# An expert step with its bias products first and the next rows' gather between the halves of gate and up

## The chip, the cores and the metric
The kernel runs on one core of a Trainium2 chip. The metric is the device time of one execution in microseconds. Of the kernel before, three timed executions gave 1781.65 us as the median (1779.54 to 1782.54). A separate, profiled execution took 1782.32 us.

## The reference
The reference is two transformer blocks over 256 tokens of width 1024, in float32. The first block mixes the tokens by four recurrent branches, normalises, and then runs a mixture of experts; the second block is a dilated attention with a pooling branch. The change touches only the experts:

```
gu = xb @ w_gu + b_gu                    # rows of one expert, 1024 -> 2048
gate, up = gu[:, :1024], gu[:, 1024:]
gate = minimum(gate, 7); up = clip(up, -7, 7)
glu = gate * sigmoid(1.702 * gate)
y = ((up + 1) * glu) @ w_down + b_down   # 1024 -> 1024
out[token] += weight * y                 # each token goes to 4 of the 32 experts
```

All 32 experts are run, each on the rows of the tokens that chose it (at most 64 rows in one step). An expert has 8 MB of gate and up weights and 4 MB of down weights, and each weight is read from HBM once.

## The kernel before, in words
The order of the work is written out by hand for each engine, with semaphores between them. TensorE (PE), VectorE (DVE), ScalarE (ACT) and SyncE's DMA queue (SP) each run their own loop over 32 expert steps `i`. Steps 0, 1 and 2 are written out on PE; steps 3 to 7, 8 to 23 and 24 to 31 are loops. Steps 8 to 23 carry an extra piece each, `embed` (line 1347), a product of the first block's gating that has nothing to do with the expert. Between steps 25 and 26 stands `expert_bias` (line 1324).

PE's step (lines 1350 to 1406) is, in its order:
1. the gate and up products, line 1360: for `k` 0 to 7, four matmuls (two banks, two column halves of the array). `k` 0 to 3 read weight room 0, `k` 4 to 7 room 1, each of 4 MB. After every second `k` the semaphore `gu_used` is raised;
2. the bias products, line 1367: four small matmuls of 32 rows that pick the expert's bias out of the table `BGU` by a one-hot `ESEL`; they close the sums and raise `gu_full`;
3. `scatter`, line 1337: the rows of the step before are added to their tokens in four banks;
4. `gather`, line 1311: the rows of the next expert are picked out of `x1` by a one-hot `PICK`, into `x_bank`;
5. two transposes of `PICKW` (line 1382), the next scatter's table;
6. four transposes of the hidden rows `GH` (line 1386), which wait for `h_ready`;
7. `turn_rows`, line 1318: four transposes of the gathered rows `XR`, into the up bank;
8. the down products, line 1399, on rooms 2 and 3 (2 MB each), which wait for `hm_ready`, and in steps 8 to 23 `embed`.

DVE's part (lines 2435 to 2455) picks the one-hots for later gathers and scatters early in the step, then waits for `gu_full` and works the activation: minimum of the gate (2443), clip of the up half (2444), the next `ESEL` (2445), the product with the sigmoid (2447), the last product (2448), which raises `h_ready`; then it copies `PTW` (2450). ACT (lines 1786 to 1800) does the sigmoid (1788), copies the gathered rows to `XR` (1790), the turned hidden rows to `HM` (1792), which raises `hm_ready`, the turned gathered rows to `XG` (1794) and the result rows to `YSB` (1796).

SP issues the four weight transfers of a step in the order of the rooms 0, 1, 2, 3, each once its room is free: room 0 when `k` 3 of the step before is done, room 1 when `k` 7 is, room 2 after the first half of the down products, room 3 after the second (line 539). In the first two refills (line 535) rooms 0 and 1 come by halves.

Of the kernel before, what the change touches and what calls it, by code (L numbers as in the profile page):

```python
# [16 lines left out]
KD = D // P  # L17
W = 512
# [6 lines left out]
EXPERTS = 32  # L25
CAP = 64
# [175 lines left out]
def build(nc, ins, consts, outs):  # L202
    stack = ExitStack()
    with stack:
# [6 lines left out]
        def sig(name):  # L211
            if name not in signals:
                signals[name] = stack.enter_context(nc.semaphore(name.replace(" ", "_")))
            return signals[name]
# [136 lines left out]
        ESEL = room(at, CAP)[0:2 * EXPERTS]; at += CAP  # L351
# [10 lines left out]
        BGU = room(at, D)[0:2 * EXPERTS]; at += D  # L362
# [20 lines left out]
        gate_bank, up_bank, y_bank, x_bank = small_bank  # L383
# [298 lines left out]
        def _(pe):  # L682
# [72 lines left out]
            for m in range(2):  # L755
                for k in range(KD):
                    if k % 4 == 0 and m == 0:
                        pe.wait_ge(sig(f"first_in_{k // 4}"), 32)
                    mm = pe.matmul(ps[:, m * T:m * T + T], w[:, k, m * P:m * P + P], XT[:, k, :], start=k == 0, stop=k == KD - 1)
# [12 lines left out]
            for nm, wt in (("gx", WX), ("ga", WAD)):  # L772
                for i in range(2):
                    ps = small(f"D {nm} {i}")
                    for m in range(2):
                        mm = pe.matmul(ps[:, m * T:m * T + T], wt[:, 2 * i + m, :], xc[:, 2 * i + m, :], start=True, stop=True)
# [7 lines left out]
            for k in range(KD):  # L784
                mm = pe.matmul(ps[0:8, 0:T], w[:, k, :], XT[:, k, :], start=k == 0, stop=k == KD - 1)
# [13 lines left out]
            for i in range(2):  # L799
                ps = small(f"C row {i}")  # L800
                for m in range(2):
                    mm = pe.matmul(ps[:, m * T:m * T + T], c("headrow", (2 * i + m) * P, (2 * i + m + 1) * P)[0:4, :], gC, start=True, stop=True)
                mm.then_inc(sig("small_full"), 1)
            ps = small("C col")
            for n, r in enumerate((uC, mC)):
                for j in range(TT):
                    mm = pe.transpose(ps[:, 8 * n + 4 * j:8 * n + 4 * j + 4], r[:, j * P:j * P + P], ident[0:4, 0:4])
# [13 lines left out]
            for j in range(TT):  # L821
                ps = small(f"C num {j}")
                for h in range(4):
                    if j == 0:
                        mm = pe.matmul(ps[:, h * P:h * P + P], sC[:, h, 0:P], vC[:, 0, h * P:h * P + P], start=True, stop=True)
                    else:
                        pe.matmul(ps[:, h * P:h * P + P], sC[:, h, P:T], vC[:, 0, h * P:h * P + P], start=True, stop=False)
                        mm = pe.matmul(ps[:, h * P:h * P + P], sC[:, h, T:T + P], vC[:, 1, h * P:h * P + P], start=False, stop=True)
                mm.then_inc(sig("small_full"), 1)
            ps = small("C den")  # L830
            for h in range(4):
                pe.matmul(ps[:, h:h + 1], sC[:, h, 0:P], c("ones", 0, 1), start=True, stop=True)
                pe.matmul(ps[:, 4 + h:5 + h], sC[:, h, P:T], c("ones", 0, 1), start=True, stop=False)
                mm = pe.matmul(ps[:, 4 + h:5 + h], sC[:, h, T:T + P], c("ones", 0, 1), start=False, stop=True)
# [31 lines left out]
            for l in range(8):  # L866
# [3 lines left out]
                elif l == 6:  # L870
                    ps = small("B level 6")
                    for n in range(8):
                        j, h = divmod(n, 4)
                        e = eBs[0][:, h, j * P:j * P + P]
                        mm = pe.matmul(ps[0:CH, n * CH:n * CH + CH], e[:, 0:CH], e[:, CH:P], start=True, stop=True)
                    mm.then_inc(sig("small_full"), 1)
                else:
                    ps = small("B cross")
                    for h in range(4):
                        mm = pe.matmul(ps[:, h * P:h * P + P], eBs[1][:, h, 0:P], eBs[1][:, h, P:T], start=True, stop=True)  # L880
# [426 lines left out]
            def gather(bank):  # L1307

                for j in range(TT):
                    for half in range(2):  # L1310
                        mm = pe.matmul(bank[CAP * half:CAP * half + CAP, :], PICK[:, j, :], x1[:, j, half * W:half * W + W],  # L1311
                                       start=j == 0, stop=j == 1, skip_group_check=True)
                return mm
# [36 lines left out]
            def expert_step(i, tile, before=None):  # L1350


                pe.wait_ge(sig("xg_ready"), i + 1)
                for k in range(KD):
                    if k % 4 == 0:
                        pe.wait_ge(sig(f"expert_in_{k // 4}"), 16 * i + 64 if before is None else 32 * i + 32)
                        w = expert_room(k // 4)
                    for n, bank in enumerate((gate_bank, up_bank)):
                        for half in range(2):
                            mm = pe.matmul(bank[CAP * half:CAP * half + CAP, :], XG[:, k % 4, k // 4, :], w[:, k % 4, n * D + half * W:n * D + half * W + W],  # L1360
                                           start=k == 0, stop=False, skip_group_check=True)
                    if k % 2:
                        mm.then_inc(sig("gu_used"), 1)
                pe.wait_ge(sig("esel_ready"), i + 1)
                for n, bank in enumerate((gate_bank, up_bank)):
                    for half in range(2):
                        mm = pe.matmul(bank[CAP * half:CAP * half + CAP, :], ESEL[EXPERTS * n:EXPERTS * n + EXPERTS],  # L1367
                                       BGU[EXPERTS * n:EXPERTS * n + EXPERTS, half * W:half * W + W], start=False, stop=True, skip_group_check=True)
                mm.then_inc(sig("gu_full"), 1)
                if before != 0:  # L1370
                    if before == 1:
                        pe.wait_ge(sig("proj_out"), proj_no("pp 3") + 1)
                    pe.wait_ge(sig("y_ready"), i)
                    pe.wait_ge(sig("ptw_ready"), i + 1)
                    scatter(first=before == 1)
                pe.wait_ge(sig("pick_ready"), i + 2)
                if tile is not None:
                    pe.wait_ge(sig("ple_sig"), i - 7)
                gather(x_bank).then_inc(sig("gathered"), 1)
                pe.wait_ge(sig("pickw_ready"), i + 1)  # L1380
                for j in range(TT):
                    mm = pe.transpose(y_bank[:, j * P:j * P + P], PICKW[:, j, :], ident)
                mm.then_inc(sig("ptw_full"), 1)
                pe.wait_ge(sig("h_ready"), i + 1)
                for m in range(4):
                    mm = pe.transpose(gate_bank[:, m * P:m * P + P], GH.rearrange("s (p k) -> s p k", k=4)[:, :, m], ident)
                mm.then_inc(sig("ht_full"), 1)
                pe.wait_ge(sig("rows_ready"), i + 1)
                turn_rows(up_bank).then_inc(sig("rows_turned"), 1)
                pe.wait_ge(sig("ptw_ready"), i + 2)  # L1390
                pe.wait_ge(sig("hm_ready"), i + 1)
                for u in range(2):
                    pe.wait_ge(sig(f"expert_in_{2 + u}"), 16 * i + 16)
                    if before == 1 and u == 0:
                        pe.wait_ge(sig("extra_in"), 16)
                    for m in range(4):
                        w = extra if before == 1 and u == 0 and m < 3 else expert_room(2 + u)
                        for half in range(2):
                            mm = pe.matmul(y_bank[CAP * half:CAP * half + CAP, :], HM[:, m, u, :], w[:, m, half * W:half * W + W],  # L1399
                                           start=u == 0 and m == 0, stop=u == 1 and m == 3, skip_group_check=True)  # L1400
                    if u == 0:
                        mm.then_inc(sig("down_used"), 1)
                mm.then_inc(sig("y_full"), 1)
                if tile is not None:
                    pe.wait_ge(sig("ple_in"), 32)
                    embed(i, tile)
# [489 lines left out]
        def _(dve):  # L1896
# [529 lines left out]
            def expert_step(i, tile):  # L2426
                link = [0]

                def then(ins_):

                    link[0] += 1
                    ins_.then_inc(sig("expert_chain"), 1)
                    dve.wait_ge(sig("expert_chain"), LINKS * i + link[0])

                e, nxt = i % EXPERTS, (i + 1) % EXPERTS
                dve.wait_ge(sig("ptw_full"), i + 1)
                pick(PICKW, e, "pickw_ready", True)
                dve.wait_ge(sig("pickw_ready"), i + 1)
                then(TS(rank[:, :, bass.ds(e, 1)], rank[:, :, bass.ds(e, 1)], -float(CAP), None, ALU.add))
                dve.wait_ge(sig("gathered"), i + 1)  # L2440
                pick(PICK, nxt, "pick_ready", False)
                dve.wait_ge(sig("gu_full"), i + 1)
                TS(GH, gate_bank[:, :], 7.0, None, ALU.min).then_inc(sig("g_ready"), 1)  # L2443
                then(TS(UH, up_bank[:, :], 7.0, -7.0, ALU.min, ALU.max))
                dve.tensor_copy(ESEL, c("eye32")[0:2 * EXPERTS, bass.ds(nxt, 1)].to_broadcast([2 * EXPERTS, CAP])).then_inc(sig("esel_ready"), 1)
                dve.wait_ge(sig("sig_ready"), i + 1)
                then(TTn(GH, GH, SGH, ALU.mult))
                STT(GH, UH, 1.0, GH, ALU.add, ALU.mult).then_inc(sig("h_ready"), 1)
                dve.wait_ge(sig("ptw_full"), i + 2)
                dve.tensor_copy(PTW, y_bank[:, 0:T]).then_inc(sig("ptw_ready"), 1)  # L2450
                assert link[0] == LINKS
                if tile is not None:
                    dve.wait_ge(sig("ple_sig"), i - 6)
                    v = base[:, tile, bass.ds((i % 8) * P, P)]
                    TTn(v, v, SGP, ALU.mult).then_inc(sig("ple_mul"), 1)  # L2455
# [198 lines left out]
```

## Time and profile before
| | us |
|---|---|
| median of the timed executions | 1781.65 |
| profiled execution | 1782.32 |
| its span, first to last instruction | 1780.5 |
| PE busy within the span | 1731.1 |
| DVE busy / ACT busy | 498.3 / 261.0 |

The expert steps run from 519.4 to 1446.7 us of the span; before them stands the first block, behind them the second block. The chain that ended last is PE for 87% of the span and DMA for 9%, the latter all transfers of gate and up weights.

How to read it: a chain of waits is followed back from the last instruction, so its pieces are the time that counts. A busy PE is not the same as PE at its peak, since its ends are modelled. Durations below come from the profiled execution.

### The profile page before, as it was taken

To read this page: it belongs to the slowest core of one execution; us is meant where nothing else is said; L and a number is where in the kernel's file an instruction comes from. 1 tells how busy PE (TensorE), PEld (TensorE's weight loads), DVE (VectorE), ACT (ScalarE), POOL (GpSimd) and SP (SyncE) were. 2 spreads that over 40 slices of the span, in tenths; PEclk is the share of its full clock that TensorE was granted. 3 is DMA by queue.
4 is the path that set the end of the run, shared out by engine and by line. 5 is a ranking of instruction groups with operands and counts; after the bars stand their busy time and mean duration, and the time that the engine had idled before them with its cause. 6 is when DMAs were issued, how large, how long until landed. Compare 5 with 4: busy or idle time off the path is not lost.

```text
span 1780.5 us, 23148 instructions
## 1 busy us (share of the span) xinstructions
PE 1731.1 (97%) x9773; PEld 993.0 (56%) x9773; DVE 498.3 (28%) x976; ACT 261.0 (15%) x433; POOL 27.3 (2%) x39
## 2 busy tenths in 40 slices
PE   8999999999999999999999999999999989999998
PEld 7677888888653333333334343433333338778884
DVE  2452367644441101011111111112011140016603
ACT  0322214000111111110101010101010121002100
POOL 1000000110000000000000000000000000000000
PEclk9999999999999999999999999999999999999999
DMA  8473333364589999999999999999999985332341
GB/s 308 180 283 118 120 119 143 94 228 179 184 329 403 433 426 434 427 435 430 430 433 428 432 428 433 429 432 430 428 431 429 430 332 213 142 142 95 139 149 38
DMA packets 51647, 539.18 MB, mean 303 GB/s; under 512 B 4078, under 2 KB 12572, under 8 KB 29568
## 3 DMA queue, kind: packets, MB, share of 16 engines
q1 hardware_dynamic: 46272, 528.25, 71.6%
q10 hardware_dynamic: 3472, 4.85, 1.0%
q0 software_dynamic: 1840, 5.14, 0.9%
q8 instruction: 51, 0.84, 0.2%
q14 instruction: 12, 0.10, 0.0%
HBM read 532.46 MB, written 5.77 MB: 302 GB/s over the span
## 4 chain that ended last, share of the span: by engine, by line
PE 87%; DMA 9%; DVE 2%; ACT 1%; issue 1%; SPq 0%; DVEq 0%; ACTq 0%
PE small L1360 22%; PE proj L710 10%; PE small L1399 10%; DMA arena<-in_expert_w_gu 9%; PE proj L1442 6%; PE proj L914 5%; PE proj L1530 4%; PE proj L1337 3%; PE small L1311 3%; PE small L1347 2%; PE small L993 2%; PE small L731 2%; PE small L1592 2%; PE proj L720 2%; PE small L1460 2%; PE small L1224 2%
## 5 line engine op out<-in xcount | busy, mean ns | idle before, releaser
L1360 PE MATMUL small<-arena 128*64 128x512 f32 x2048 | 449.2, 595 | 12.8 <-DMA arena<-in_expert_w_gu 10.4
L1360 PEld LDWEIGHTS small<-arena 128*64 128x64 f32 x2048 | 150.2, 137 | 296.4 <-issue 275.6
L1399 PE MATMUL small<-arena 128*64 128x512 f32 x1024 | 226.8, 595 | 8.6 <-ACT arena L1792 8.1
L710 PE MATMUL proj<-arena 128*128 128x256 f32 x832 | 186.5, 385 | 0.0
L2443 DVE TENSOR_SCALAR arena<-small 128x512 f32<-128x512 f32 x32 | 22.1, 692 | 546.2 <-PE small L1367 546.2
L710 PEld LDWEIGHTS proj<-arena 128*128 128x128 f32 x832 | 159.3, 193 | 25.4 <-issue 3.0
L1399 PEld LDWEIGHTS small<-arena 128*64 128x64 f32 x1024 | 74.2, 137 | 139.2 <-issue 139.2
L1613 ACT ACTIVATE arena<-proj 128x512 f32<-128x512 f32 x95 | 55.8, 596 | 516.7 <-PE proj L710 149.7
L1442 PE MATMUL proj<-arena 128*128 128x256 f32 x512 | 111.1, 379 | 0.0
L1442 PEld LDWEIGHTS proj<-arena 128*128 128x128 f32 x512 | 97.2, 190 | 13.7 <-issue 0.5
L1788 ACT ACTIVATE arena<-arena 128x512 f32<-128x512 f32 x32 | 20.2, 630 | 498.2 <-DVE arena L2443 498.2
L914 PE MATMUL proj<-arena 128*128 128x256 f32 x384 | 88.9, 388 | 0.0
L914 PEld LDWEIGHTS proj<-arena 128*128 128x128 f32 x384 | 72.6, 193 | 10.3
L1530 PE MATMUL proj<-arena 128*128 128x256 f32 x320 | 71.5, 381 | 0.6 <-DVE arena L2529 0.6
L1530 PEld LDWEIGHTS proj<-arena 128*128 128x128 f32 x320 | 59.9, 190 | 9.3 <-issue 1.1
L1337 PE MATMUL proj<-arena 64*128 64x512 f32 x256 | 63.6, 615 | 0.7 <-ACTq L1811 0.7
L1311 PE MATMUL small<-arena 128*64 128x512 f32 x264 | 63.9, 605 | 0.1
L2455 DVE TENSOR_TENSOR arena<-arena 128x128 f32 x16 | 4.7, 293 | 167.9 <-ACT arena L1800 167.9
L1796 ACT ACTIVATE arena<-small 128x512 f32<-128x512 f32 x32 | 19.1, 597 | 216.5 <-PE small L1399 216.5
L2529 DVE TENSOR_TENSOR arena<-proj,arena 128x512 f32<-128x512 f32 (+2 forms) x24 | 13.4, 558 | 121.0 <-PE proj L1509 118.8
L1337 PEld LDWEIGHTS proj<-arena 64*128 64x128 f32 x256 | 22.0, 186 | 41.9 <-issue 40.2
L1311 PEld LDWEIGHTS small<-arena 128*64 128x64 f32 x264 | 16.0, 136 | 43.6 <-issue 43.2
(451 smaller groups left out, 1528.2 us busy)
## 6 DMA issues: line engine op xcount, KB each, us to landing
arena<-in_expert_w_gu SPq DMA_DIRECT2D x58, 4096.0 KB, 18.9
arena<-in_expert_w_down SPq DMA_DIRECT2D x63, 2048.0 KB, 15.6
arena<-in_w_in_first SPq DMA_DIRECT2D x20, 2048.0 KB, 7.8
arena<-in_w_in SPq DMA_DIRECT2D x16, 2048.0 KB, 7.9
arena<-in_expert_w_gu SPq DMA_DIRECT2D x12, 2048.0 KB, 11.7
arena<-in_w_ada SPq DMA_DIRECT2D x6, 2048.0 KB, 9.5
arena<-in_w_branch SPq DMA_DIRECT2D x4, 2048.0 KB, 8.9
arena<-in_w_out SPq DMA_DIRECT2D x4, 2048.0 KB, 7.9
```

The costliest lines, as they stand in the source:

```text
L710: mm = pe.matmul(ps[:, m * T:m * T + T], w[:, k, (2 * b + m) * P:(2 * b + m + 1) * P], XT[:, k, :], start=k == 0, stop=k == KD - 1)
L720: mm = pe.matmul(ps[:, :], XT[:, k, j * P:j * P + P], w[:, k, :], start=k == 0, stop=k == KD - 1)
L731: mm = pe.matmul(ps[:, m * T:m * T + T], w[:, k, (2 * i + m) * P:(2 * i + m + 1) * P], YT[b][:, k, :], start=k == 0, stop=k == KW - 1)
L914: mm = pe.matmul(ps[:, m * T:m * T + T], w[:, k, quarter * P:quarter * P + P], XT[:, k, :], start=k == 0, stop=k == KD - 1)
L993: mm = pe.matmul(ps[:, m * T:m * T + T], w[:, k, (2 * i + m) * P:(2 * i + m + 1) * P], YT[b][:, k, :], start=k == 0, stop=k == KW - 1)
L1311: mm = pe.matmul(bank[CAP * half:CAP * half + CAP, :], PICK[:, j, :], x1[:, j, half * W:half * W + W], start=j == 0, stop=j == 1, skip_gro ...
L1337: mm = pe.matmul(acc_bank[2 * j + half][:, :], PTW[lo:lo + CAP, j * P:j * P + P], YSB[lo:lo + CAP, :], start=first, stop=False, skip_group ...
L1360: mm = pe.matmul(bank[CAP * half:CAP * half + CAP, :], XG[:, k % 4, k // 4, :], w[:, k % 4, n * D + half * W:n * D + half * W + W], start= ...
L1399: mm = pe.matmul(y_bank[CAP * half:CAP * half + CAP, :], HM[:, m, u, :], w[:, m, half * W:half * W + W], start=u == 0 and m == 0, stop=u = ...
L1442: mm = pe.matmul(ps[:, m * T:m * T + T], w[:, k, (2 * b + m) * P:(2 * b + m + 1) * P], HT[:, k, :], start=k == 0, stop=k == KD - 1)
L1530: mm = pe.matmul(ps[:, m * T:m * T + T], w[:, k, (2 * b + m) * P:(2 * b + m + 1) * P], HT[:, k, :], start=k == 0, stop=k == KD - 1)
L1613: act.activation(dst, v, func).then_inc(sig("proj_out"), 1)
```

## The change
The four bias products come first in the step and open the sums (start=True); the gate and up products follow, and `k` 7 closes them. The gather of the next rows stands between `k` 3 and `k` 4. The semaphore `gu_full` is gone: DVE waits for the fourth `gu_used` of the step instead. Everything else of the step stays: scatter, PICKW transposes, hidden rows, gathered rows, down products.

```diff
                 pe.wait_ge(sig("xg_ready"), i + 1)
+                pe.wait_ge(sig("esel_ready"), i + 1)
+                for n, bank in enumerate((gate_bank, up_bank)):
+                    for half in range(2):
+                        pe.matmul(bank[CAP * half:CAP * half + CAP, :], ESEL[EXPERTS * n:EXPERTS * n + EXPERTS],
+                                  BGU[EXPERTS * n:EXPERTS * n + EXPERTS, half * W:half * W + W], start=True, stop=False, skip_group_check=True)
                 for k in range(KD):
+                    if k == 4:
+                        pe.wait_ge(sig("pick_ready"), i + 2)
+                        if tile is not None:
+                            pe.wait_ge(sig("ple_sig"), i - 7)
+                        gather(x_bank).then_inc(sig("gathered"), 1)
                     if k % 4 == 0:
                         pe.wait_ge(sig(f"expert_in_{k // 4}"), 16 * i + 64 if before is None else 32 * i + 32)
                         w = expert_room(k // 4)
...
-                                           start=k == 0, stop=False, skip_group_check=True)
+                                           start=False, stop=k == KD - 1, skip_group_check=True)
                     if k % 2:
                         mm.then_inc(sig("gu_used"), 1)
-                pe.wait_ge(sig("esel_ready"), i + 1)
-                for n, bank in enumerate((gate_bank, up_bank)):
-                    for half in range(2):
-                        mm = pe.matmul(bank[CAP * half:CAP * half + CAP, :], ESEL[EXPERTS * n:EXPERTS * n + EXPERTS],
-                                       BGU[EXPERTS * n:EXPERTS * n + EXPERTS, half * W:half * W + W], start=False, stop=True, skip_group_check=True)
-                mm.then_inc(sig("gu_full"), 1)
                 if before != 0:
                     if before == 1:
                         pe.wait_ge(sig("proj_out"), proj_no("pp 3") + 1)
                     pe.wait_ge(sig("y_ready"), i)
                     pe.wait_ge(sig("ptw_ready"), i + 1)
                     scatter(first=before == 1)
-                pe.wait_ge(sig("pick_ready"), i + 2)
-                if tile is not None:
-                    pe.wait_ge(sig("ple_sig"), i - 7)
-                gather(x_bank).then_inc(sig("gathered"), 1)
                 pe.wait_ge(sig("pickw_ready"), i + 1)
...
-                dve.wait_ge(sig("gu_full"), i + 1)
+                dve.wait_ge(sig("gu_used"), 4 * i + 4)
```

## Rows read from the trace of the kernel before
**Rows 1.** The page: busy time of each engine, share of span, instructions
```profile
PE 1731.1 (97%) x9773; PEld 993.0 (56%) x9773; DVE 498.3 (28%) x976; ACT 261.0 (15%) x433; POOL 27.3 (2%) x39
```
**Rows 2.** A window: PE, PEld, DVE, ACT, POOL busy; granted clock, DMA share, GB/s
```profile
1200.00:1300.00 100.00, 97.36 (x462) 35.96 (x456) 20.57 (x48) 11.75 (x20) 1.08 (x2) 0.98 1.01 430
```
**Rows 3.** Chain, step 15, with embed: start us, length us, what
```profile
949.76 13.88 PE small L1360 x64
963.64 1.02 PE small L1367 x8
964.66 1.92 PE proj L1337 x8
966.58 1.87 PE small L1311 x8
968.45 0.37 PE small L1382 x2
968.82 0.49 PE small L1386 x4
...
969.33 0.61 ACT arena L1792
...
970.17 7.09 PE small L1399 x32
977.26 1.98 PE small L1347 x16
979.24 13.88 PE small L1360 x64
```
**Rows 4.** Chain, step 0, where nothing covers the hidden rows
```profile
519.38 13.95 PE small L1360 x64
533.34 1.06 PE small L1367 x8
...
537.41 0.75 PE small L1386 x4
...
538.90 7.09 PE small L1399 x32
545.99 13.73 PE small L1360 x64
```
**Rows 5.** Timeline: engine, line, shape, count, idle before and its releaser
```profile
536.15 0.44 PE L1382 MATMUL small<-arena 128*128 128x128 f32 x2
...
951.83 0.42 DVE L2409 TENSOR_SCALAR arena<-arena 128x64 f32<-128x64 f32 x2 [0.16 <-DVE arena L2439]
...
957.04 0.14 PEld L1360 LDWEIGHTS small<-arena 128*64 128x64 f32 x2 [0.29 <-issue]
...
963.57 0.21 PEld L1367 LDWEIGHTS small<-arena 32*64 32x64 f32 x8 [0.81 <-issue]
```
**Rows 6.** Chain: step starts 3 and 4, the transfer-paced steps, step 9
```profile
600.40 13.73 PE small L1360 x64
...
627.75 13.75 PE small L1360 x64
...
641.69 20.80 DMA arena<-in_expert_w_gu
...
720.98 7.11 PE small L1360 x32
...
750.20 7.09 PE small L1360 x32
...
772.88 13.88 PE small L1360 x64
```
**Rows 7.** Chain: steps 26 and 28 and the last one's end
```profile
1275.15 15.58 PE small L1360 x64
...
1331.70 13.75 PE small L1360 x64
...
1425.97 7.09 PE small L1360 x32
...
1446.69 0.02 issue
```

## What the change does to the time
> **What bounds the kernel now.** I read the page first. PE is busy for 97% of the span [rows 1], so a saving or a stall on PE can count; but this busy share doesn't tell whether PE or the weights set the pace of the expert steps. The windows do: in the expert stretch the DMA engines are busy all the time at 430 GB/s [rows 2]. A step's weights are 12.58 MB, so the transfers need 12.58 / 0.430 = 29.26 us for each step.
>
> Then the chain of waits. A step with embed takes 979.24 - 949.76 = 29.48 us, all of it on PE but for one wait for the copy of the hidden rows [rows 3]. A step without embed takes 627.75 - 600.40 = 27.35 us where PE runs free [rows 6]; the first two full ones take 27.20 each, as the two together and step 3 fill 627.75 - 545.99 = 81.76 us [rows 4, 6]. In steps 5 to 8 PE waits at k = 4 for room 1, and these waits end 750.20 - 720.98 = 29.22 us apart [rows 6], the pace of the DMA engines. So three phases: PE first, transfers in steps 5 to 8, PE in the embed steps 9 to 23 (0.26 us a step slower than the transfers), then PE again without embed until it has caught up, and transfers for the last three steps (the wait of step 31 ends at 1425.97 [rows 7]). Pace and PE lie close together: where the change shortens a transfer-paced step nothing is won, and where it lengthens one, up to 29.22 - 27.35 = 1.87 us is free.
>
> **The change part by part.** Two reorderings, and what they uncover.
>
> The work of PE. No matmul is added or removed. The bias products cost 1.02 [rows 3] wherever they stand. Most groups carry about 0.15 us on entry if the tile shape changes: the gate and up products take 13.88 after embed (128x128) [rows 3] and 13.73 after the down products, which have their own shape 128x64 [rows 6]; the weight load of the bias products waits 0.81 instead of 0.29 [rows 5]. Now gate and up follow the bias products' 32x64 in every step: 13.88 always, 0.15 more than 13.73 without embed. The gather has the shape of its new neighbours: its 8 instructions run in pairs, and a pair of this shape takes 0.14 + 0.29 = 0.43 us (weight load and idle time before it [rows 5]), so 4 x 0.43 = 1.72, against 1.87 where it stands now [rows 3]. A gather amid gate and up stands nowhere in this trace. Bounds: 1.72, and 1.87 + 0.15 = 2.02 if both borders cost. I take 1.72, since down to gate and up is the nearest row of two groups of one shape, and it costs nothing.
> The Trainium skill, "TensorEngine Tiling (Array Packing)", Tiling Modes, Key Properties, says that changing the tiling mode drains the engine, while changing the tile within it doesn't. By it the gather costs 1.72; with 2.02 the sum below would be 32 x 0.30 = 9.6 us more.
>
> The waits put ahead of k = 4 (pick_ready, ple_sig, and the transfer's own): the picks end 2.5 us into the step (951.83 + 0.42 - 949.76) [rows 3, 5], the gather comes 1.02 + 7.02 = 8.0 us into it, so they hold nobody; behind them in PE's queue stand the gather and the second half. A satisfied wait costs nothing: the weight load at k = 4, 957.04, comes after the usual 0.29 us [rows 5]. The dropped gu_full and the wait for gu_used come at the same matmul, the last of k = 7. ACT copies the gathered rows after the sigmoid, while DVE makes its two last products; that stays hidden.
>
> What the gather and the bias products covered. DVE and ACT can begin the activation only when the sums are closed, and PE needs the hidden rows for the transposes of line 1386. Step 0 shows how long this takes, since nothing is scattered there: the sums close at 534.40, the transposes start at 537.41, 3.01 us later [rows 4]. In step 15 the sums close at 964.66, and scatter 1.92, gather 1.87 and the PICKW transposes 0.37 make 4.16 us of cover [rows 3]: 1.15 to spare. After the change only scatter and PICKW are left: 1.92 + 0.37 = 2.29. PE stalls 3.01 - 2.29 = 0.72 us in every step. From the first such transpose to the down products it is 970.17 - 968.82 = 1.35 in a running PE [rows 3], and 538.90 - 537.41 = 1.49 after an idle PE [rows 4]. PE now comes from idle, so I take 1.49; 1.35 is the lower end.
>
> The sum of one step: 1.02 + 13.88 + 1.72 + 3.01 + 1.49 + 7.09 = 28.21 us without embed, + 1.98 = 30.19 with it. Against before: +1.01 in steps 1 and 2, +0.86 from 27.35, +0.71 from 29.48. Step 0 had 1.06 + 13.95 + 3.01 + 1.49 ahead of its down products with the gather wholly hidden in the 3.01. It becomes 1.02 + 13.88 + 1.72 + 3.01 + 1.49 = 21.12 against 538.90 - 519.38 = 19.52 [rows 4]: +1.60.
>
> The transfers. SP issues them in order; a release that moves later could idle the engines. Room 0 is released about 1.1 us later in the step (bias and the 0.15), room 1 2.8 later (gather too), rooms 2 and 3 as far ahead of the step's end as before. The needs move as well, room 0's by 1.02 and room 1's by 1.02 + 0.08 + 1.72 = 2.8, so the time from release to need doesn't shrink. It is 30.19 + 9.76 - 16.6 = 23.3 us for room 1, where a transfer from issue to landing with the whole backlog took 20.80 [rows 6]. The stream as a whole starts later with the end of step 0, 1.60 us. So the room 1 of step 8, landed at 750.2 before [rows 6], lands at 751.8.
>
> Is PE late enough that it never waits? Step 4 starts at 627.75 + 1.60 + 2 x 1.01 + 0.86 = 632.2, step 8 at 632.2 + 4 x 28.21 = 745.1, and its k = 4 is due at 745.1 + 9.76 = 754.9, 3.1 us after the landing. From there PE only falls further behind (30.19 against 29.22, 16 times), and in the last 8 steps wins back 1.01 each. So all transfer waits go, PE paces everything, and the waits of before are a credit.
>
> Step by step against the chain of before:
> - up to step 4: 1.60 + 1.01 + 1.01 + 0.86 = +4.5
> - steps 4 to 8: before 772.88 - 627.75 = 145.1 with its waits [rows 6], after 4 x 28.21 + 30.19 = 143.0: -2.1
> - steps 9 to 23: 15 x 0.71 = +10.7
> - steps 24 to 27: 4 x 0.86 = +3.4
> - steps 28 to 31: before 1446.69 - 1331.70 = 115.0 [rows 7], after 4 x 28.21 = 112.8: -2.2
>
> Sum +14.3 us. Behind the last step the same chain follows; its two ada weight transfers are issued when the last gate and up are done, 4.50 + 7.09 = 11.6 us ahead of the end of the last down products, and by then no expert weights stand before them (4.2 MB, 9.8 us at 430 GB/s). Against the profiled execution: 1782.3 + 14.3 = 1796.6; its median stands 0.7 below, so 1795.9.
>
> **The rivals.**
> *Transfers set the pace and the stall is free (not slower).* Then only the ends count: after the last landing of room 1, 1446.69 - 1425.97 = 20.7 us follow now [rows 7]. The bias and the gather (2.9 us) would lie before that landing, and the stream starts 1.60 later: -1.3, 1780.4. It decides this way if PE's lead lasts, that is if the chain of activation takes less than the 2.29 of cover, so that a step with embed stays near 29.4. Against it: 3.01 us in [rows 4]. 5%.
> *The transfer waits don't go.* If the later releases delay the landings as much as PE is late, the credits fall away: 1.6 + 2 x 1.01 + 6 x 0.86 + 16 x 0.71 + 7 x 0.86 = 26.2, so 1807.8. Against it: 23.3 us of window, 20.80 for a landing [rows 6]. 5%.
> *The gather costs at both borders*, 0.30 a step: 1795.9 + 9.6 = 1805.5. 5%.
> *PE's clock falls in the stall.* In the window from 1200 us the granted clock is 0.98 [rows 2]: behind the 3.63 us of expert_bias, gate and up took 15.58 instead of 13.88, partly at 1.2 GHz [rows 7], 1.7 us lost. Between scatter and the down products there are now 0.37 + 0.72 + 1.49 = 2.6 us of transposes and idling, against 1.7 before. In step 0 of before it was 538.90 - 536.15 = 2.75, and the down products behind it took their full-speed 7.09 [rows 4, 5]. So every step: 3%, 1.7 x 31 = 53 us, 1849. In step 0 alone, where 4.5 us of it come together, it may happen: 1.7 more, within the range.
> The Trainium skill, "TensorE: Matmul & The Clock Gate", Part 4, holds that transposes don't count as busy for the clock gate. By that the 2.6 us are idle throughout; the result is this rival's.
> *The change doesn't do what it says:* the gather holds up the second half since its one-hots are late. The 5.5 us between picks and gather speak against it. 2%, some 1800 to 1810.
>
> **How the numbers follow.** Forecast, PE paces all with 0.72 us of stall: 80%. Each 0.1 us of a step is 3.2 us in all. Lower end of my bounds: 1.35 instead of 1.49, -4.5; with some wait of steps 5 to 8 coming back no more than that. Upper end: half of the gather's borders +4.8, the clock in step 0 +1.7. Range 1790 to 1802.5. About 0.2% (3.6 us) is what a measurement of this kernel tells from no change. Slower by more: the forecast and all rivals but the first, 0.94; within: 0.04 from the first rival; faster 0.02, if that one's ends gain more than I worked out.
>
> **What would show it.** Chain: steps with embed 30.2 us long, all others 28.2, the same to the end, with no DMA piece from step 5 on. Line 1386 on PE is waited for from DVE's line 2448 in all 32 steps, 0.7 us each. Line 1311 takes 1.72. Line 1360 holds no wait for in_expert_w_gu. DMA share falls a little below 1.00 in steps 9 to 31. It would be wrong if the transposes follow PICKW without idling, if a DMA wait stands in the last steps, or if the windows show a granted clock below 0.99 in many steps.

## The result, and the profile after

The changed kernel takes 1803.22 us (four executions, 1802.84 to 1803.51) against 1782.08: 1.0126 times the kernel before, with an interval of 1.0113 to 1.0138. That is 21.1 us slower, where 14.3 were forecast, and 0.7 us above the range. The profiled execution has a span of 1801.7 us; its expert steps begin at 519.39, where they began at 519.38 before, and end at 1467.80 instead of 1446.69, so all of the 21.1 us arise there.

An embed step of the changed kernel, by the chain of waits (start us, length us, what), the answer to [rows 3]:

```profile
960.65 1.02 PE small L1357 x8
961.67 7.02 PE small L1370 x32
968.69 1.72 PE small L1311 x8
970.40 6.89 PE small L1370 x32
977.30 0.02 issue
...
977.93 0.69 DVE arena L2444
...
978.86 0.69 DVE arena L2447
...
979.57 0.70 DVE arena L2448
...
980.32 0.76 PE small L1386 x4
...
981.10 0.61 ACT arena L1792
981.71 0.23 issue
981.94 7.09 PE small L1399 x32
989.03 1.98 PE small L1347 x16
991.01 1.02 PE small L1357 x8
```

In [rows 3] the chain stays on PE through scatter, gather and both transposes. Here it leaves PE at the end of the up products, 977.30, and comes back at 980.32: DVE's activation stands on the path. Scatter and the PICKW transposes still run, but beside it. The step takes 991.01 - 960.65 = 30.36 us instead of 29.48. The list of waits says it for all 32 steps (engine, line waited for: us in total, times, longest):

```profile
PE small L1386 <- DVE arena L2448: 26.2, 32, 2.7
PE small L1399 <- ACT arena L1792: 11.4, 29, 0.4
```

In the kernel before, line 1386 waited for DVE only in step 0 [rows 4]. PE's wait for weights, which paced steps 5 to 8 and the last three [rows 6, 7], has shrunk to one piece of the chain, in step 8:

```profile
735.68 21.97 DMA arena<-in_expert_w_gu
...
757.70 7.11 PE small L1370 x32
```

And step 0 answers to [rows 4] like this:

```profile
539.13 1.13 PE small L1386 x4
540.26 0.85 PE small L1318 x4
541.11 7.78 PE small L1399 x32
548.89 1.02 PE small L1357 x8
```

The transposes and the down products took 9.76 us instead of 8.58: part of them ran at 1.2 GHz in this execution, as the windows show (PE, PEld, DVE, ACT, POOL busy; granted clock, DMA share, GB/s). The clock falls behind 2.68 us in which PE had nothing to do but wait for line 2448.

```profile
540.00:545.00 5.00, 5.00 (x22) 2.08 (x22) 0.54 (x3) 1.19 (x2) 0.00 (x0) 0.74 1.01 433
```

### The profile page after: what moved, and what is told of

Read it like the earlier page. It is cut to its first block, busy times and chain, and to the rows that moved or that the text cites. A ratio compares the mean times of both kernels' runs of the same rounds, so it can differ in the third digit from the quotient of the medians.

```text
span 1801.7 us, 23209 instructions
## 1 busy us (share of the span) xinstructions
PE 1733.3 (96%) x9773; PEld 989.6 (55%) x9773; DVE 494.0 (27%) x976; ACT 254.1 (14%) x433; POOL 27.2 (2%) x39
## 4 chain that ended last, share of the span: by engine, by line
PE 89%; DVE 5%; issue 2%; DMA 2%; ACT 1%; DVEq 0%; SPq 0%; ACTq 0%
PE small L1370 24%; PE small L1399 12%; PE proj L710 10%; PE proj L1442 6%; PE proj L914 5%; PE proj L1530 4%; PE small L1311 3%; PE small L1347 2%; PE small L1357 2%; PE small L993 2%; PE small L731 2%; PE small L1592 2%; PE proj L720 2%; PE small L1460 2%; PE small L1224 2%
## 5 line engine op out<-in xcount | busy, mean ns | idle before, releaser
L1370 PEld LDWEIGHTS small<-arena 128*64 128x64 f32 x2048 | 144.5, 137 | 302.4 <-issue 300.8
L1399 PE MATMUL small<-arena 128*64 128x512 f32 x1024 | 227.6, 597 | 11.9 <-ACT arena L1792 11.4
L1399 PEld LDWEIGHTS small<-arena 128*64 128x64 f32 x1024 | 73.7, 137 | 143.7 <-issue 143.7
L1386 PE MATMUL small<-arena 128*128 128x128 f32 x128 | 24.4, 314 | 26.2 <-DVE arena L2448 26.2
```

## The experiments

Theory A: the gather and the bias products were the cover of the activation; without them PE stalls in every step, and that stall is the loss. Rival B: the later release of the weight rooms delays the transfers. Rival C: the gather amid the products, or the bias ahead of them, costs by itself. Behind each time stands its ratio to the kernel before, timed beside it, with the 95% interval in brackets.

### bias_first: the bias products alone
Against the changed kernel:
```diff
                 for k in range(KD):
-                    if k == 4:
-                        pe.wait_ge(sig("pick_ready"), i + 2)
-                        if tile is not None:
-                            pe.wait_ge(sig("ple_sig"), i - 7)
-                        gather(x_bank).then_inc(sig("gathered"), 1)
...
                     scatter(first=before == 1)
+                pe.wait_ge(sig("pick_ready"), i + 2)
+                if tile is not None:
+                    pe.wait_ge(sig("ple_sig"), i - 7)
+                gather(x_bank).then_inc(sig("gathered"), 1)
```


> Only the bias products move to the front; the gather stays behind scatter. Theory A (the loss is the activation that lost its cover): scatter 1.92, gather 1.87 and PICKW 0.37 still cover 3.02 us, so line 1386 is waited for only in step 0, embed steps stay at 29.5 us, the others go to 27.5 (0.15 for the entry from another tile shape), the last steps are paced by the transfers, and 1.02 us less stands behind the last landing: 1780 to 1783. Theory B (the loss is the later release of the weight rooms): rooms 0 and 1 are released 1.1 us later in each step, which would cost some 5 us or more of the 21: 1787 or above.

Measured: 1780.94 us, 1.0002 (0.9993 to 1.0011). No change. Its chain has the gather behind scatter again, and the transposes of line 1386 (here 1385) follow on PE's own order:

```profile
993.20 1.92 PE proj L1337 x8
995.12 1.87 PE small L1311 x8
996.98 0.37 PE small L1381 x2
997.35 0.49 PE small L1385 x4
```

So bias first costs nothing in the sum, though rooms 0 and 1 are released some 1.1 us later in each step. (The steps without embed do take 27.50 us instead of 27.35, for gate and up enter from another tile shape. That is paid for where PE waited for weights.)

### gather_mid: the gather alone
The same lines moved the other way in the kernel before, where the bias products stay behind the products:
```diff
                 for k in range(KD):
+                    if k == 4:
+                        pe.wait_ge(sig("pick_ready"), i + 2)
...
+                        gather(x_bank).then_inc(sig("gathered"), 1)
...
                     scatter(first=before == 1)
-                pe.wait_ge(sig("pick_ready"), i + 2)
...
-                gather(x_bank).then_inc(sig("gathered"), 1)
```


> Only the gather moves between the halves; the bias products close the sums as before. Theory A: cover is 2.29 us for 3.02, a stall of 0.75 us in every step and 1.63 from the first transpose to the down products; 28.2 us without embed and 30.3 with it, so +18 to +20 over before: 1800 to 1802. Theory B: room 0 is released no later than before, room 1 by 1.7: less than half of the loss, 1792 or below.

Measured: 1799.24 us, 1.0107 (1.0091 to 1.0122), 18.9 us over before: most of the loss, by this one move. The step without embed takes 28.24 us here and 28.38 in the changed kernel, and 15 times 0.14 is most of the difference between the two. Its chain leaves PE behind the bias products at 972.16 and comes back at 975.19, 3.03 us later:

```profile
971.10 1.06 PE small L1372 x8
972.16 0.02 issue
...
975.19 0.76 PE small L1387 x4
```

### gate_early: both moves, but a shorter activation behind the products
Against the changed kernel, on PE and then on DVE. In the second half (k 4 to 7) all gate products come first, then all up products:
```diff
+                    if k > 4:
+                        continue
                     for n, bank in enumerate((gate_bank, up_bank)):
-                        for half in range(2):
...
+                        for kk in (range(4, KD) if k == 4 else (k,)):
+                            for half in range(2):
...
+                        if k == 4 and n == 0:
+                            mm.then_inc(sig("gate_full"), 1)
...
-                dve.wait_ge(sig("gu_used"), 4 * i + 4)
+                dve.wait_ge(sig("gate_full"), i + 1)
                 TS(GH, gate_bank[:, :], 7.0, None, ALU.min).then_inc(sig("g_ready"), 1)
-                then(TS(UH, up_bank[:, :], 7.0, -7.0, ALU.min, ALU.max))
...
                 dve.wait_ge(sig("sig_ready"), i + 1)
                 then(TTn(GH, GH, SGH, ALU.mult))
+                dve.wait_ge(sig("gu_used"), 4 * i + 4)
+                then(TS(UH, up_bank[:, :], 7.0, -7.0, ALU.min, ALU.max))
                 STT(GH, UH, 1.0, GH, ALU.add, ALU.mult).then_inc(sig("h_ready"), 1)
```


> The changed kernel, but in the second half of gate and up the gate products of k 4 to 7 come first, then the up products, and DVE works the gate, with the sigmoid, while the up products run. Behind the last up product stand only the clip (0.69) and the last product (0.70), 1.5 us, less than the 2.29 us of cover. Theory A: no stall at line 1386, the steps take 27.4 and 29.4 us, and the whole loss goes: 1778 to 1782. Theory B (releases) and C (the gather in mid costs by itself): releases and gather are as in the changed kernel, so it stays at 1795 or above.

Measured: 1779.87 us, 0.9997 (0.9988 to 1.0006). The whole loss is gone, with bias first, the gather between the halves, and the rooms released as late as in the changed kernel. That speaks against B and C at once. Its step, by the chain:

```profile
959.04 6.87 PE small L1373 x32
965.90 1.92 PE proj L1337 x8
967.82 0.37 PE small L1387 x2
968.19 0.49 PE small L1391 x4
...
976.63 1.98 PE small L1347 x16
978.61 1.02 PE small L1357 x8
```

From the products to the transposes all stands on PE. The step before this piece begins with its bias products at 949.28, so it is 978.61 - 949.28 = 29.33 us long.

### before_more1, before_more2, before_more4: the kernel before, its activation made longer
The added line stands n times behind the clip of the up half, n = 1, 2, 4, and LINKS is 3 + n:
```diff
                 then(TS(UH, up_bank[:, :], 7.0, -7.0, ALU.min, ALU.max))
+                then(TS(UH, UH, 7.0, -7.0, ALU.min, ALU.max))
```


> The kernel before with one DVE operation more in the activation: the clip of the up half is done twice (0.7 us, same values). Theory A: 3.7 us of activation under 4.16 us of cover, hidden in every step but step 0, where nothing covers it: +0 to +1 us. If the length of the activation counted whatever the cover, it would be 32 x 0.7 = +22 us.

Measured: 1780.35 us, 0.9996 (0.9986 to 1.0005). Hidden, as expected.

> The kernel before with two such operations more: 4.45 us against 4.16 of cover. Theory A: PE now stalls 0.3 us in a step, and its restart after idling costs 0.27 more (1.63 instead of 1.36 from the first transpose to the down products): +0.56 a step. Transfers still pace the steps up to 8, then 23 x 0.56 = 12.9 less the 5.6 us of waits that end in the last steps, and 1.4 in step 0: +7 to +10 us. Without a threshold: +45 us.

Measured: 1782.99 us, 1.0008 (0.9999 to 1.0018), +1.7 us against the median of before beside it. The expectation missed, by its own price: a clip from memory to memory takes 0.44 us, not the 0.69 of the one that reads the bank. So the activation was 3.01 + 2 x 0.47 = 3.95 us and stayed under the 4.16 of cover. PE comes to its very edge here: it doesn't stall, but the transposes of the hidden rows take 0.60 us in the loops instead of 0.50, since their weight loads no longer run ahead (the first begins at 824.87, 0.06 us behind DVE's last product).

```profile
824.66 0.37 PE small L1382 x2
825.03 0.60 PE small L1386 x4
```

> The kernel before, order untouched, with four more clips of the up half in the activation. The traces of before_more1 and after_more1 show 0.47 us for each (0.44 and 0.03), not 0.7, so the activation is 3.01 + 1.88 = 4.9 us against 4.16 of cover: a stall of 0.73 us a step, as in the changed kernel, with its restart (1.63 from the first transpose to the down products instead of 1.36). Theory A, the stall alone makes the loss: steps of 28.3 and 30.5 us, 1.9 + 31 x 1.0 less the 11.9 us of transfer waits that go, +20 to +22 us, the loss of the changed kernel without its reordering (1801 to 1804). If releases, the gather amid the products or the bias ahead of them had a part in the loss, this kernel loses less: +15 or below.

Measured: 1802.73 us, 1.0128 (1.0111 to 1.0145). The order of the kernel before, with the gather and the bias where they were, loses as much as the changed kernel does (1.0126) once the activation outlasts its cover by the same 0.73 us. Its step begins at 959.69 and is 990.20 - 959.69 = 30.51 us long. In this execution the clock fell in step 0 too (down products 8.78 us), so up to 1.7 us of the 22.3 below may be that. The chain:

```profile
973.58 1.06 PE small L1367 x8
974.64 0.02 issue
...
975.99 0.44 DVE arena L2445
...
979.51 0.76 PE small L1386 x4
...
990.20 10.01 PE small L1360 x45
```

The three together show the threshold: +0.47 and +0.94 us of activation cost nothing that counts, +1.88 costs 22.3 us.

### after_more1: the changed kernel, one clip more
The same edit with n = 1 on the changed kernel.

> The changed kernel with one such operation more. Theory A: the activation stands uncovered on the path in every step, so all of it counts: 32 x 0.72 = +23 us over the changed kernel, some +45 over the kernel before (about 1825). If the changed kernel were bound by transfers or releases: within 5 us of the changed kernel.

Measured: 1826.1 us, 1.0248 (1.0231 to 1.0265), 22.9 us above the changed kernel. What is free in the kernel before is paid in full here. The number of the expectation was met for a wrong reason: the clip adds 0.47 us a step, 32 x 0.47 = 15 us. The rest goes with PE's clock. In the chain, the down products of one step take 8.78 us instead of 7.09, and in the window in which they run the granted clock is 0.83 on average, part of it at 1.2 GHz and part at 2.4. In all, six steps of the loops have down products of 8.72 or 8.78 us, some 10 us in this execution:

```profile
901.56 8.78 PE small L1399 x32
```
```profile
900.00:910.00 10.00, 9.61 (x40) 3.67 (x40) 0.22 (x1) 1.09 (x2) 0.00 (x0) 0.83 0.94 405
```

Of the windows of 10 us behind step 1, seven show a clock of 0.83 to 0.95, beside one behind expert_bias; in the changed kernel the one behind expert_bias is all there is.

### after_step0: the gather of step 0 put back
Against the changed kernel:
```diff
-                    if k == 4:
+                    if k == 4 and before != 0:
...
+                if before == 0:
+                    pe.wait_ge(sig("pick_ready"), i + 2)
...
+                    gather(x_bank).then_inc(sig("gathered"), 1)
                 pe.wait_ge(sig("pickw_ready"), i + 1)
```


> The changed kernel, but in step 0 alone the gather comes behind the up products, where it stands before. Theory A with PE as the pace to the end: step 0 gives back the gather's 1.72 us and the 1.2 us of its half clock, and the wait of step 8 (0.7 to 0.9) goes: 3 to 4 us less than the changed kernel, about +18 over the kernel before. If the clock stays low there: 2 us less.

Measured: 1798.09 us, 1.0096 (1.0079 to 1.0113), against 1.0126: 0.3%, some 5 us less; the two intervals just touch. The spans of the traces differ by 6.6 us, but only part of that comes from the edit:

```profile
517.16 1.09 PE small L1357 x8
518.25 15.61 PE small L1370 x64
...
536.87 0.75 PE small L1391 x4
...
538.36 7.09 PE small L1404 x32
545.45 1.02 PE small L1357 x8
```

Step 0 ends at 545.45 instead of 548.89, but it also begins at 517.16 instead of 519.39, for the first block took less time in this execution. The step itself takes 28.29 us instead of 29.50, 1.2 less. Its down products ran at full clock, but its gate and up products lost 1.7 us, at a granted clock of 0.82 from 520 to 525 us. Line 1370 has no DMA piece left among the waits, which gives 0.9. The step behind expert_bias is 1.7 us shorter, since its gate and up products kept full clock here (the first half 7.02 us, against 8.71 in the trace of the changed kernel), and the edit doesn't touch that. So losses of 1.7 us by the clock come and go between executions. Without them the edit is worth 1.2 + 1.7 + 0.9 = 3.8 us, an estimate from these rows that agrees with the expectation; the rest of the 5 is not explained.

### before_light, after_light: no step paced by transfers
From step 3 on each weight transfer brings only three of its four rows, in the kernel before and in the changed one. Both leave out a quarter of the weights, so they don't compute what the reference does; only their times are used.
```diff
             with sp.Fori(3, n_steps) as i:
+                def expert(e, u):
+                    sp.dma_start(expert_room(u)[:, 0:3, :], expert_unit(e, u)[0][:, 0:3, :]).then_inc(sig(f"expert_in_{u}"), 16)
```


> The kernel before with lighter transfers: from step 3 on each weight transfer carries only three of its four rows per partition, so a quarter of each room keeps an older expert's weights. No step can be paced by transfers any more. It gives what the transfer waits cost before: 6.25 us in steps 4 to 8 and 5.6 in 28 to 31, so -10 to -12.5 us (about 1769).

Measured: 1768.25 us, 0.9928 (0.9913 to 0.9943), -12.9 us.

> The changed kernel with the same lighter transfers (a quarter of each room keeps an older expert's weights from step 3 on). Theory A: the changed kernel is paced by PE from step 1 on and has one wait of 0.9 us left, so -0.5 to -1.5 us: +20 over the kernel before. Theory B (late transfers carry the loss): it falls to the time of the kernel before or below.

Measured: 1801.93 us, 1.0119 (1.0104 to 1.0135), 1.3 us below the changed kernel. The transfers cost the kernel before 12.9 us and the changed one next to nothing; theory B would have had it the other way about. PE's own work and waits have grown by 1801.93 - 1768.25 = 33.7 us, and 21 of it show, since 12 fell into time in which PE waited for weights anyway.

after_light shows one thing more. Its step 0 is that of the changed kernel, with the same stall of PE, but its down products (line 1401 here) kept full clock in this execution, 7.09 us instead of 7.78:

```profile
538.01 0.75 PE small L1388 x4
538.76 0.48 PE small L1320 x4
...
539.50 7.09 PE small L1401 x32
```

### turn_first and turn_first_start: what the order is worth at its best
Against gate_early, the hidden rows' transposes (line 1386) come ahead of PICKW's (1382):
```diff
+                pe.wait_ge(sig("h_ready"), i + 1)
...
+                mm.then_inc(sig("ht_full"), 1)
                 pe.wait_ge(sig("pickw_ready"), i + 1)
...
                 mm.then_inc(sig("ptw_full"), 1)
-                pe.wait_ge(sig("h_ready"), i + 1)
...
-                mm.then_inc(sig("ht_full"), 1)
```


> As gate_early, and the transposes of the hidden rows come ahead of those of PICKW, so that the copy of the hidden rows (0.61 + 0.23 us, until now idle time of PE) runs beside PICKW's and the gathered rows' transposes. Theory A: 1.5 us of activation under 1.92 of scatter; a step loses 0.37 us more, 27.0 and 29.0 us, both under the 29.22 of the transfers, which now pace all steps from the fifth on: 1774 to 1779, faster than before. If PE's order doesn't matter any more beside the transfers: the same as gate_early.

Measured: 1779.12 us, 0.9993 (0.9984 to 1.0002). That is at the upper edge of what was expected and not told apart from gate_early or from the kernel before: the gain didn't show. PE's steps did get shorter (27.18 us from 626.27 to 653.45, in step 4), and the chain holds ten DMA pieces instead of the five of gate_early (two of them below). With its steps faster than the weights arrive, PE only waits more.

```profile
1346.06 21.87 DMA arena<-in_expert_w_gu
1375.28 21.86 DMA arena<-in_expert_w_gu
```

turn_first_start, against turn_first:
```diff
-                    if k == 4:
+                    if k == 4 and before not in (0, 1):
...
+                if before in (0, 1):
+                    pe.wait_ge(sig("pick_ready"), i + 2)
...
+                    gather(x_bank).then_inc(sig("gathered"), 1)
                 pe.wait_ge(sig("h_ready"), i + 1)
```


> As turn_first, but in steps 0 and 1 the gather stands behind the up products (step 0) or scatter (step 1): in step 0 it covers the activation, and the step ends 1.5 us earlier, so the stream of transfers, which paces all later steps, starts 1.5 us earlier; in step 1 room 1 is released 1.7 us earlier. 1.5 to 3 us less than turn_first: 1776 to 1778. If the start of the stream is bound by something else: the same as turn_first.

Measured: 1777.52 us, 0.998 (0.9971 to 0.9989): faster than both kernels, by 3.6 us against the median of before beside it. Step 0 now takes 544.48 - 519.29 = 25.19 us instead of 545.02 - 518.24 = 26.78 in turn_first, 1.6 less, though it ends only 0.5 earlier, since it began 1.05 later in this execution. The last DMA piece of the chain starts at 1403.11 instead of 1404.49, 1.4 us earlier, and that is the gain between the two profiled executions. What is left is the stream of the weights.

```profile
1403.11 21.88 DMA arena<-in_expert_w_gu
...
1425.03 7.09 PE small L1373 x32
1432.12 1.92 PE proj L1337 x8
1434.04 0.68 PE small L1392 x4
```

## Why the prediction came out as it did

The mechanism was right, and each of its halves was tested: the activation lost its cover (gate_early takes the loss away, before_more4 makes it without the reordering), and PE became the pace (before_light, after_light). The direction was right; the size was not: the terms below add 7.1 us to the sum of 14.3, and the time lay outside the range. The step that failed is the 1.49 us taken for the way from the first transpose to the down products, where 1.62 to 1.63 was measured. Point by point:

- *Gather 1.72, gate and up 13.88, activation 3.01, stall 0.72.* Measured 1.72, 7.02 + 6.89 = 13.91, 980.32 - 977.30 = 3.02. Right. The gather's borders cost nothing: the Trainium skill, "TensorEngine Tiling (Array Packing)", Tiling Modes, Key Properties (a change of the tiling mode drains the engine, a change of tile doesn't) is borne out here. That rival falls. (The stall by itself is 0.76 us a step in the list of waits, behind step 0.)
- *1.49 from the first transpose to the down products.* This is the step that failed most. It measured 981.94 - 980.32 = 1.62. I took it from step 0 [rows 4], since PE came from idling there, and gave 1.35 as the other end. But step 0 is written out, and from step 3 on the steps are loops: there the copy of the hidden rows (0.61) is followed by 970.17 - 969.94 = 0.23 us before the down products [rows 3], and behind an idle PE the transposes release it after 0.75 [rows 4] instead of 0.49. The two rows had to be put together: 0.75 + 0.02 + 0.61 + 0.23 = 1.61, and 1.62 to 1.63 was measured. Both ends of my bound lay below the truth. With 0.03 of gate and up it is 0.17 a step, 29 x 0.17 = 4.9 us of the 7.1.
- *Step 0, +1.60.* Measured 548.89 - 545.99 = +2.90. The 1.3 more are the clock, which I had seen as possible there and left out of the sum. It isn't a fixed price: the same step 0 takes 546.58 - 518.28 = 28.30 us in after_light, at full clock, 1.69 over the 26.61 of before, and in gather_mid too the down products of step 0 take 7.09 behind an uncovered activation. What decides it from one execution to the next stays open, and so does how many of the timed executions had it.
- *The clock falls in every step.* The steps in the loops of the changed kernel have 2.7 us of transposes and stall between scatter and the down products, and these take 7.09: that rival falls. It begins to be true with 0.47 us more, in six steps of after_more1. By the Trainium skill, "TensorE: Matmul & The Clock Gate", Part 4, transposes don't count as work for the clock as other matmuls do. after_more1 is in line with it, for in the step shown PE idles for only 1.6 of the 3.2 us between scatter and the down products, and the rest are transposes; but no run here separates the two.
- *Room 1 of step 8 lands at 751.8, so PE never waits.* It landed at 757.66, 7.5 us later than before. PE waited 0.71 us for it, and its second half took 7.11 instead of 6.89: 0.9 together. The window of 23.3 us from release to need was worked out with the 30.19 us of a step with embed. Steps 5 to 8 begin behind steps without it, and the same sum gives 28.21 + 9.76 - 16.6 = 21.4 us, less than the 21.97 that the transfer took in the chain above. So the rival in which waits stay had more for it than I saw. The stream also started 2.9 us late with step 0, not 1.6, and lost more at its start: from 545 to 550 us it ran at 147 GB/s, where the kernel before had 240, and from 550 to 560 at 374 against 431. In step 1 room 0's first half is issued at 553.53, 4.1 us later than the 549.45 of before, with little left in the queue. These rows don't account for all of the 7.5 us.
- *The credits.* Waits of 6.25 us (145.13 - 4 x 27.35 - 29.48) and 5.6 us (114.99 - 4 x 27.35) were taken as gone: 11.9. before_light measured 12.9, after_light left 1.3 in the changed kernel. Right but for the 0.9 of step 8, and the rival in which all the waits stay falls.
- *The transfers as pace, the stall free.* It needed an activation under 2.29 us of cover. gate_early has that, and measured 0.9997: this rival was right about what would happen beyond its point, and wrong that the kernel lay beyond it.

Summed up: 14.3 + 4.9 + 1.3 + 0.9 = 21.4, against 21.1 by the end of the expert steps. With the 4.9 alone the forecast would have been 1800.8; the 1.3 and the 0.9, which the profiled execution had, lead from there to the 1803.

## What to carry to other kernels

Before work is moved on the bounding engine, add up what stands between a result and its use: here 4.16 us of it covered 3.02 us of DVE and ACT, and the move took 1.87 of it and left 2.29. That step 0 showed the 3.02 uncovered was worth more than any sum of durations; but a row of a step written out isn't the price of a step in a loop, and a stall's price is the stall plus the restart behind it. Where two paces lie within a few per cent, a loss on one is partly paid by waits for the other (12 of 33 us here), and a gain on it is soon taken up by them: the best order found wins 3.6 us, and got clear of the noise only when a shorter step 0 let the stream of the weights start earlier.

## What the runs showed of the hardware

- The same clip of 128x512 float32 on DVE takes 0.69 us when it reads the matmul's bank and 0.44 when it reads and writes SBUF. The Trainium skill, "VectorE: DVE Perf Modes", Why PSUM operands drop a tier, explains it: a bank in PSUM gives DVE one read port, and the faster mode for float32 needs both ports of SBUF.
- A stall on PE costs about 0.27 us more than its own length: from the first transpose to the down products 1.62 behind an idle PE, 1.35 in a running one. With no stall but the result only just ready (before_more2), it is 0.10 us.
- Half a microsecond more of waiting in each step let the granted clock fall in six of after_more1's steps in the loops and not in others, with 1.7 us lost in each, so that kernel lost 23 us for 15 us of waiting. The same code may lose such 1.7 us in one execution and not in the next: so the products behind expert_bias (8.71 us for the first half in the changed kernel, 7.02 in after_step0).
